# Sample attention: the value pages are issued by GpSimd in a loop of its own, and SyncE issues the key pages alone

## What is computed

```python
k_past = cache_k[page_table].reshape(db, past_len, N_HEADS, 2, HEAD_DK)
v_past = cache_v[page_table].reshape(db, past_len, N_HEADS, HEAD_DV)
s_past = jnp.einsum('bqhmd,bkhmd->bhmqk', q, k_past) * ATTN_SCALE
s_new = jnp.einsum('bqhmd,bkhmd->bhmqk', q, k_new) * ATTN_SCALE      # causal
p = jax.nn.softmax(jnp.concatenate([s_past, s_new], axis=-1), axis=-1)
w = p[:, :, 0] - lam * p[:, :, 1]
o = einsum(w[..., :P], v_past) + einsum(w[..., P:], v_new)
```

## Time and profile before

| | |
|---|---|
| median of 3 runs | 2319.48 us (2319.07 to 2324.77) |
| the profiled execution | 2321.42 us, span of its records 2319.4 us |
| mean granted TensorE clock | 0.861 |
| TensorE busy | 1923.5 us, 83% |
| VectorE, ScalarE, GpSimd busy | 812.2, 727.6, 201.5 us |
| sample attention | about 1370 to 1763 us of the span |
| pages issued by SyncE | 128 of keys, 128 of values, 512 KB each |

### The profile page before, as it was taken

How to read it: one execution, slowest core, us unless ns; L and a number is a source line. 1 busy time by engine, 2 the same in 40 slices (tenths; PEclk the granted TensorE clock), 3 DMA queues, 4 the chain that set the end, 5 groups by cost and what they waited for, 6 DMA issues and landing times.

```text
span 2319.4 us, 46887 instructions
## 1 busy us (share of the span) xinstructions
PE 1923.5 (83%) x18265; PEld 1715.5 (74%) x18265; DVE 812.2 (35%) x1399; ACT 727.6 (31%) x1055; POOL 201.5 (9%) x333
## 2 busy tenths in 40 slices
PE   4524787696999999969797679888877969999998
PEld 3324566595999999959794347766653969999998
DVE  3843600334323232341375852222222332323322
ACT  2123000423333331232334336434412133333222
POOL 0611000022000001120101110000001310000000
PEclk6556557697999999979897779998986979999999
DMA  8596987621222222212203029998984212222222
GB/s 193 130 145 96 247 229 186 195 82 45 73 81 81 81 68 85 78 52 83 61 19 118 0 92 334 386 368 326 378 313 155 70 39 76 87 81 77 71 86 71
DMA packets 384074, 315.30 MB, mean 136 GB/s; under 512 B 45148, under 2 KB 345672, under 8 KB 383880
## 3 DMA queue, kind: packets, MB, share of 16 engines
q1 hardware_dynamic: 342376, 288.94, 39.5%
q10 hardware_dynamic: 41328, 24.42, 5.5%
q0 software_dynamic: 256, 0.26, 0.0%
HBM read 300.96 MB, written 12.62 MB: 135 GB/s over the span
## 4 chain that ended last, share of the span: by engine, by line
PE 63%; DMA 11%; DVE 7%; issue 6%; SPq 4%; ACT 3%; ACTq 2%; POOL 2%; DVEq 0%; POOLq 0%
PE ps L549 49%; DMA kpg<-in_cache_k 4%; PE ps L459 3%; SPq L409 2%; DMA raw<-in_w_ada_ffn 2%; SPq L416 2%; PE ps L495 2%; DMA raw<-in_w_ada_mix 1%; PE ps L734 1%; DMA vpg<-in_cache_v 1%; ACTq L1063 1%; PE ps L683 1%; PE ps L830 1%; PE ps L643 1%; PE ps L482 1%
## 5 line engine op out<-in xcount | busy, mean ns | idle before, releaser
L549 PE MATMUL ps<-hr,ws 128*128 128x288 f32 x6528 | 908.6, 302 | 74.4 <-DVE hr L1643 74.3
L549 PEld LDWEIGHTS ps<-hr,ws 128*128 128x128 f32 x6528 | 897.0, 194 | 87.0 <-issue 47.6
L1637 DVE TENSOR_TENSOR ws<-raw,ws 128x1024 fp32r<-128x1024 f32 x200 | 234.7, 1174 | 743.0 <-ACT ws L1094 743.0
L1094 ACT ACTIVATE ws<-raw 128x1024 fp32r<-128x1024 f32 x200 | 201.6, 1009 | 710.6 <-PE ps L549 653.2
L549 PE MATMUL ps<-gr,ws 128*128 128x288 f32 x2112 | 281.9, 296 | 0.0
L549 PEld LDWEIGHTS ps<-gr,ws 128*128 128x128 f32 x2112 | 281.7, 189 | 0.0
L1256 ACT ACTIVATE kTs<-ps 128x512 f32<-128x512 f32 x256 | 139.4, 597 | 178.7 <-PE ps L459 178.5
L495 PE MATMUL ps<-raw,cond 128*32 128x128 f32 x1792 | 108.8, 398 | 83.9 <-issue 36.7
L459 PE MATMUL ps<-ident,kpg 128*128 128x128 f32 x1024 | 145.0, 288 | 35.5 <-DMA kpg<-in_cache_k 34.3
L459 PEld LDWEIGHTS ps<-ident,kpg 128*128 128x128 f32 x1024 | 117.4, 146 | 59.9 <-ACT kTs L1256 29.0
L495 PEld LDWEIGHTS ps<-raw,cond 128*32 128x32 f32 x1792 | 66.5, 152 | 97.5 <-issue 65.7
(11 more groups left out here) (283 smaller groups left out, 1619.4 us busy)
## 6 DMA issues: line engine op xcount, KB each, us to landing
kpg<-in_cache_k SPq DMA_DIRECT2D x128, 512.0 KB, 5.9
vpg<-in_cache_v SPq DMA_DIRECT2D x128, 512.0 KB, 6.0
raw<-in_ffn_w SPq DMA_DIRECT2D x88, 512.0 KB, 3.7
raw<-in_w_ada_mix SPq DMA_DIRECT2D x48, 512.0 KB, 5.9
raw<-in_w_ada_ffn SPq DMA_DIRECT2D x48, 512.0 KB, 6.0
raw<-in_ffn_w SPq DMA_DIRECT2D x48, 384.0 KB, 3.3
raw<-in_w_ada_kv SPq DMA_DIRECT2D x16, 512.0 KB, 5.9
raw<-in_ssm_w_glu SPq DMA_DIRECT2D x16, 512.0 KB, 4.0
```

Source lines behind the costliest of these rows:

```text
L549: last = mm(ps[:, 4 * s + 2 * tile + h, 0:HALF], ws[:, wslot, w, k, :], src[:, k0 + k, v, h * HALF:(h + 1) * HALF], start=first, stop=(end ...
L1094: A(ws[:, w, 0, 0:nk, :].rearrange("p k n -> p (k n)"), raw[:, slot, 0:nk, :].rearrange("p k n -> p (k n)"), ACT.Copy).then_inc(slab_high, 1)
L1637: TT(f(ws[:, w, 1, 0:nk, :]), f(raw[:, slot, 0:nk, :]), f(ws[:, w, 0, 0:nk, :]).bitcast(F32), ALU.subtract).then_inc(raw_done[slot], 1)
```

## The change

SyncE's loop issues key pages alone: turns 0 to 7, 128 issues, then at once the slabs of `wo`. The value pages are issued by GpSimd with the same waits and the same slots: after `new_values(0)` the sixteen pages of sequence 0, after each `new_keys(b)` those of sequence b - 2, and after `new_values` 6 and 7 those of 6 and 7. The loop has four turns of four pages. Nothing else differs; the transfers and what is computed are the same.

```diff
-            def page_loads(b, o, u, keys, values):
+            def key_page(b, o, u):
                 slot = u % 4
-                for go, seq, cache, dst, ready in ((keys, b, "cache_k", kpg, k_full), (values, b - LAG, "cache_v", vpg, v_full)):
...
+                at = b * PAGES + o * 8 + u
+                page = sp.value_load(pages[0:1, ds(at, 1)], min_val=0, max_val=NPOOL - 1)
+                if not isinstance(at, int) or at > 3:
+                    sp.wait_ge(k_turned, at * 2 - 6)
+                sp.dma_start(kpg[:, slot]..., a["cache_k"][ds(page, 1)]...).then_inc(k_full[slot], 16)
...
                 for u in range(PAGES):
-                    page_loads(0, u // 8, u % 8, True, False)
-                def loads(b, keys=True, values=True):
+                    key_page(0, u // 8, u % 8)
+                with sp.Fori(1, DB) as b:
                     with sp.Fori(0, PAGES // 8) as o:
                         for u in range(8):
-                            page_loads(b, o, u, keys, values)
-                for b in range(1, LAG):
-                    loads(b, values=False)
-                with sp.Fori(LAG, DB) as b:
-                    loads(b)
-                for b in range(DB, DB + LAG):
-                    loads(b, keys=False)
+                            key_page(b, o, u)
                 slabs("wo", one)
...
+            def value_pages(b):
+                with pool.Fori(0, PAGES // 4) as o:
+                    for u in range(4):
+                        at = b * PAGES + o * 4 + u
+                        page = pool.value_load(pages[0:1, ds(at, 1)], min_val=0, max_val=NPOOL - 1)
+                        pool.wait_ge(v_used, at + 1)
+                        pool.dma_start(vpg[:, u]..., a["cache_v"][ds(page, 1)]...).then_inc(v_full[u], 16)
             for b in range(NBUF):
                 new_keys(b, b)
             new_values(0)
+            value_pages(0)
             for b in range(NBUF, DB):
                 new_values(b - LAG)
                 pool.wait_ge(new_scored, b - NBUF + 1)
                 new_keys(b, b % NBUF)
+                value_pages(b - LAG)
             for b in range(DB - LAG, DB):
                 new_values(b)
+                value_pages(b)
```

More of the change, by code:

```diff
@@ L400, in long @@
                 return i * (2 * P) + (j // 4) * P
-            def page_loads(b, o, u, keys, values):
+            def key_page(b, o, u):
                 slot = u % 4
-                for go, seq, cache, dst, ready in ((keys, b, "cache_k", kpg, k_full), (values, b - LAG, "cache_v", vpg, v_full)):
[L406 to L417, removed]
+                at = b * PAGES + o * 8 + u
+                page = sp.value_load(pages[0:1, ds(at, 1)], min_val=0, max_val=NPOOL - 1)
+                if not isinstance(at, int) or at > 3:
+                    sp.wait_ge(k_turned, at * 2 - 6)
+                sp.dma_start(kpg[:, slot].rearrange("p h m -> p (h m)"), a["cache_k"][ds(page, 1)].rearrange("o k h m d -> k (o h m d)")
+                             ).then_inc(k_full[slot], 16)
             slabs("ada0", one)
@@ L1468, in new_values @@
                 pool.dma_start(vn[:, :], out[9][ds(b, 1)].rearrange("b t h d -> t (b h d)")).then_inc(vn_full, 16)
+            def value_pages(b):
[4 more added lines that the diff above has]
+                        pool.wait_ge(v_used, at + 1)
+                        pool.dma_start(vpg[:, u].rearrange("p h m -> p (h m)"), a["cache_v"][ds(page, 1)].rearrange("o k h d -> k (o h d)")
+                                       ).then_inc(v_full[u], 16)
             for b in range(NBUF):
```

## The result

The changed kernel takes 2356.8 us (2347.2 to 2363.1, 4 runs) against 2319.3 for the kernel before: ratio 1.0143, 95% interval 1.0106 to 1.0181. It is slower, as forecast, but by 37 us, not by 18. Its profiled execution took 2363.1 us with a span of 2361.2.

What follows compares the result with a forecast made beforehand. It took the DMA engines to bound full turns. Its terms, 2.7 - 3 + 2 - 0.5 + 16.5 = +17.7 us on 2319.5, gave 2337 us; own range 2328 to 2357, stated range 2308 to 2372.

Steps and rivals of the forecast that it cites:

- low case for turns 8 and 9: Value-only turns 8 and 9 with GpSimd at the lower pace, 1.28 us a page: 26.4 us a turn, -3.1 together.
- a sign of being wrong: Prediction wrong if turns 8 and 9 stay below 31 us or turns 3 to 7 leave 44 to 48.
- Bound by the DMA engines in full turns: Turns loading 32 pages: DMA engines bind at 408 GB/s, 1.28 us a page, 41.1 us; SyncE's freed issues gain nothing.
- GpSimd's issue: Each value page issued by GpSimd: 1.0 us for the DMA, pace 1.9 us; bounds 0.52 and 2.3 us.
- GpSimd becomes the bound: Rival, turns 3 to 9: GpSimd's pace above 2.56 us; 2447 us at pace 3.2; chance 0.10.
- Turns 8 and 9, +16.5: Value-only turns: page 0 lands at 5.6 us, then 15 paces of 1.9: 36.2 us a turn, +8.9 and +7.6.
- Turns 3, 4, 6, +2.7: Full turns: values start late, 29 pages due until value page 15 lands; 46.7 us against 45.8, +0.9 each.
- Turn 5, -3: Its 5.05 us TensorE start covers GpSimd's late start while value pages 0 to 3 load: -3 (0 to -5).
- Turn 7, +2: SyncE loads four wo slabs in front of value pages 14 and 15, 5.1 us of DMA time: +2 (0 to +5).
- Turns 0 to 2, -0.5: Sequence 0's value pages 0 to 3 load in turn 0, +1.5; turn 2 has four fewer, -2.
- The cheap issue: Rival, boundaries of turns 3 to 9: GpSimd's pace about 1.3 us makes the kernel faster, 12.5 us, 2307; chance 0.25.
- VectorE's hold on GpSimd: Rival: VectorE's weight scaling, 8 times 1.29 us, delays GpSimd's issues; 10.3 us on top of the forecast, 2347; chance 0.06.

Runs made afterwards that it cites:

- e2: Kernel before, all pages by SyncE, but value pages 0 to 3 of the next sequence held until the turn's last new-values matmul: 2331.4 us, ratio 1.0043.
- e1: Changed kernel, but GpSimd issues the next sequence's first four value pages before waiting for the last new-values matmul: 2328.8 us, ratio 1.0037.
- e3: Kernel before, but the value pages of turns 8 and 9 alone issued by GpSimd, in the changed kernel's order: 2334.1 us, ratio 1.0069.
- e5: Changed kernel, but SyncE holds the next sequence's key pages 0 to 3 until value page 13 is multiplied: 2346.9 us, ratio 1.0122.
- e8: Changed kernel, but GpSimd copies the next keys before the boundary wait and issues value pages 0 to 3 before the new-values load: 2351.0 us, ratio 1.0118.
- e9: Changed kernel with the changes of e8 and e5 together: 2339.0 us, ratio 1.0073.
- e10: e9, but every key page also waits for the value page four before it, with the key loop written out: 2363.4 us, ratio 1.0202.
- e4: Changed kernel, but VectorE's scaling of the weights written as a tensor product with a broadcast column: 2349.6 us, ratio 1.0141.
- e6: Changed kernel with eight value slots instead of four, GpSimd issuing values eight pages ahead across the boundary, wo slabs loaded last: 2312.6 us, ratio 0.9963.

## Why the prediction was right, and where it was off

The kernel is slower and the time lies in the stated range, but much of that was luck. With the pace that was measured, 1.3 us, the prediction's own low case for turns 8 and 9 (-3.1) applies, and its sum is then 2.7 - 3 + 2 - 0.5 - 3.1 = -1.9 us: no change. The kernel was slower all the same, through terms that the sum had put too low. The own range, 2328 to 2357, was said to come from a pace of 1.6 to 2.2; by 3 us for each 0.1 that gives 2328 to 2346, and the measured 2356.8 is outside it. And a sign of being wrong came true: turns 3 to 7 left 44 to 48 (49.3 to 51.3).

*Bound by the DMA engines in full turns.* Right for the middle of a turn, where the share is still 1.03 at 407 GB/s, and wrong for the changed turn as a whole: turn 3's share fell from 1.00 to 0.85. With SyncE free of 128 issues nothing was gained. The rule of the Trainium skill (DMA: Bandwidth & Descriptors, "Issuing engines are not separate DMA queues"), that issuing from several engines saves only sequencer time, agrees.

*GpSimd's issue.* Off: 0.53 us and not 1.0, pace 1.3 us and not 1.9. It is the lower bound that I had set from the earlier trace rows, practically unchanged from 32 packets to 144. The rival that GpSimd becomes the bound is excluded.

*Turns 8 and 9, +16.5.* Measured +15.8 (35.1 and 36.5), but the working was wrong twice and the errors cancelled. The pace isn't 1.9. And the low case, which a pace of 1.3 calls for, put 3.1 us of landing into a slot's round, where the earlier trace rows has 5.18 and these turns now have 5.2 in the median. With 5.2 the round is (1.1 + 0.15 + 0.5 + 5.2) / 4 = 1.7 us a page, and no longer under the DMA engines' 1.28. By the runs the two causes are a start without cover, some 4 us a turn (e2: +7.7), and GpSimd as the issuer without a hole (e1: +5.5). e3 measured both: +13.4. The changed kernel has 2.4 us more. In its turn 9 the load of the new values started 2.9 us after the matmul that it waits for (1770.19, after 1767.3; 0.3 us in e3), with no releaser shown; that is left open. The granted clock fell too, from 0.75 and 0.62 in the two turns to 0.56 and 0.50. A value page's matmuls are part of a slot's round, so some of each term may be the clock; no run takes it apart. The kernel before in turns 3, 8 and 9:

```profile
1472.30:1518.50 46.20, 39.53 (x702) 32.15 (x701) 11.61 (x24) 19.30 (x34) 1.61 (x6) 0.95 1.00 382
...
1705.20:1732.50 27.30, 17.99 (x294) 10.33 (x293) 5.48 (x12) 2.10 (x2) 0.52 (x1) 0.75 0.83 287
1732.50:1761.10 28.60, 20.51 (x293) 12.19 (x293) 3.70 (x7) 0.00 (x0) 3.52 (x4) 0.62 0.87 298
```

*Turns 3, 4, 6, +2.7; measured +13.* This is the step that failed: "from there 29 pages are due until value page 15 has landed", and with it "the lighter last four pages mostly give back". It takes for granted that pages are served in the order in which they are issued. With one queue the sum holds: e2, which has the hole and one queue, gave the turn that this step had worked out, 46.7 us (46.8, 46.4, 45.7). With two queues the next turn's keys, which have four slots of cover, are issued beside the last values, which have none; then nothing is left to load in the hole. 32 pages instead of 29 make 3.8 us a turn, by an estimate of 1.28 us a page. e5 took the keys away from there and e8 the late start, 1.5 us a turn each in the profile and neither of them clear by its time; with both (e9) the time fell by some 17 us, which is clear. The sharing alone isn't the cost: in e1 keys and values are issued side by side too, and with the hole closed turns 3, 4, 6 and 7 took 46.9, 46.1, 45.3 and 44.0. A similar wait sits at a turn's start, where value page 1 took 6 us to land; e10 removed most such waits and lost elsewhere, so their price isn't shown.

*Turn 5, -3; measured -1.1.* The right sign: TensorE's start, 2.94 us this time instead of 5.05, covers GpSimd's.

*Turn 7, +2; measured +6.* SyncE issued the first wo slab at 1719.1, 13 us before the turn's end, as said. No keys follow this turn, so the slabs may do here what the next keys do elsewhere. They cost nothing by themselves: e1 issues them in turn 7 too (from 1698.4) and, with the hole closed, took 44.0 us for it. Their share beside the hole wasn't tried.

*Turns 0 to 2, -0.5; measured +4.* Turn 2 starts with its values loaded, but the last values stood beside the next keys here too, and turn 2 took 45.3 us instead of 41.9. This turn has no late start, so it shows the failed step by itself: without the hold on the next keys it took 45.3, 44.6 (e4) and 42.7 us (e8), with the hold 41.0 and 41.0 (e5, e9). These are single executions, and the code of the kernel before took 41.9 and 43.5 (e3).

*The rivals.* The cheap issue did come true (pace 1.3, the point from which I said it decides is 1.5), and the kernel was slower all the same, because of GpSimd's order at the boundary and of the order between the queues, whose costs the rival's sum had left at the forecast's values. VectorE's hold on GpSimd (Trainium skill, SBUF - State Buffer, "SBUF: two separate sides") is in the trace, in the five issues named at e4, and e4 found no cost that could be measured.

## What to carry to other kernels

Before a stream is moved to another engine, write down what that engine waits for between two of its transfers: here a wait for the end of the turn stood in between, and moving four issues ahead of it gave back three quarters of the loss. Splitting one queue in two also gives up the order in which transfers are needed. Here that and GpSimd's late start together cost 3 to 4 us a turn where a hole followed, since the stream with slots to spare had run ahead and left nothing to load in the hole; where the other stream ran on (e1) it cost nothing that could be seen in full turns. Eight value slots gave the two lowest medians, 0.3 to 0.4% below the kernel before, with one issuer or with two; only e6's interval ends under 1.

## What was not expected

A page of 144 packets costs GpSimd no more to issue than a load of 32: 0.53 and 0.52 us. And the kernel before spreads far more than its first three runs said: 2319.1 to 2324.8 there, 2298 to 2335 over the 22 runs beside e1 to e4. So effects under some 8 us need many runs, and the prediction's 7 us for "no change" was too narrow for single runs.
